# Another order and other PSUM banks in the attention loop of a hybrid decoder step (RetNet, RWKV-7, memory attention, MoE)

## The chip, the cores and the metric

One NeuronCore of one Trainium2 chip runs the whole program. The metric is the device time in microseconds of one execution; the kernel before is given by the median of three runs.

## What is computed

One decoder layer serves a prompt of 1024 tokens and 64 sample tokens (8 sequences of 8), model width 1024, all in float32. The change touches one of its stages, the attention over a memory of 256 tokens with 4 heads of 256, and what leads from there into the expert router:

```python
h = h + rmsnorm(h, g_mem_q) -> q @ w_mq, scores with mem_k * 256 ** -0.5, softmax, @ mem_v, @ w_mo
hn = rmsnorm(h, g_ffn)
gl = hn @ w_group_router + b_group_router        # 4 columns
el = hn @ w_expert_router + b_expert_router      # 32 columns
```

The prompt rows use keys and values projected from the prompt's memory; the sample rows use a cache of their own. Before this stage stand the combined projection and the two mixers, behind it the sorting of tokens by expert, the 32 experts and the sum of their outputs.

## The kernel before, in words

The program is a row of phases, each with engine programs written out by hand that are held together by semaphores: phase_project, phase_mixers, phase_attention, phase_route, phase_experts, phase_combine. A program for an engine runs in its written order; `wait_ge` holds the whole engine. PSUM is one tensor of eight banks; a 128 x 1024 float32 result takes two.

phase_attention (L1254 to L1983) first projects keys and values of the memory, multiplies the mixers' output by w_out, and then goes over the rows in tiles of 128: i = 0 to 7 are the prompt (NT = 8), i = 8 is the sample tile (TILES = 9). Large products with weights are made from float32 split into two halves that TensorE takes at a higher rate: ScalarE writes the high half (a_hi, o_hi), VectorE the rest (a_lo, o_lo), and TensorE adds three products (`terms`, L1759), 48 matmuls of 512 columns for each tile.

The steps of the loop over i, by the functions of the engines:
- scores(i) (L1835, TensorE): queries of tile i against kT, into banks 4 and 5.
- maxima(i) (L1500, VectorE), exps(i) (L1676, ScalarE), divide(i) (L1509, VectorE): the softmax into p.
- queries(i + 1) (L1815, TensorE): tile i + 1 times w_mq into banks 2 and 3. query_rows (L1659, ScalarE) scales them into the buffer rows; turn_q (L1827, TensorE) transposes them into banks 4 and 5; query_turned (L1668, ScalarE) copies them to qT.
- turn_p(i) (L1844, TensorE) transposes p into banks 0 and 1; p_turned(i) (L1685, ScalarE) copies it to bT.
- values(i) (L1852, TensorE): values by p, into banks 6 and 7. o_high (L1691, ScalarE) and o_low (L1514, VectorE) split the result.
- attend(i) (L1870, TensorE): times w_mo, into banks 2 and 3.
- back(i) (L1529, VectorE): adds it to h (L1532), takes the mean square (L1462, L1463), waits for POOL's reciprocal root (L1427) and writes the normed rows hn (L1539).
- turn_hn, hn_turned, router, logits (L1860, L1518, L1864, L1523) for tile i - 1, one iteration late: TensorE transposes hn into banks 0 and 1, VectorE copies it to bT (L1521), TensorE multiplies by the router's 36 columns (L1867) into bank 0, VectorE adds the bias (L1527).
- turn_h(i + 2) (L1804, TensorE), h_high (L1650, ScalarE), h_low (L1495, VectorE), front(i + 2) (L1486, VectorE): the next but one tile of h, turned into banks 4 and 5 and split, and its mean square.

All transposes are recorded at one line, L1756, in `turn`. bT serves both p and hn; qT holds the queries alone. SP's queue (L1393 to L1407) stores h (store_h2), stores hn (store_hn), loads the h of tile i + 3 (load_h1, L1329) and stores the logits of tile i - 1, in this order; behind queries(8) it asks for the cached sample keys (L1403).

TensorE's order in the loop is the one that the change rewrites:

```python
for i in range(NT):
    scores(i); queries(i + 1); turn_p(i); turn_q(i + 1); values(i)
    if i >= 1: turn_hn(i - 1)
    if i + 2 < TILES: turn_h(i + 2)
    if i >= 1: router(i - 1)
    attend(i)
```

VectorE's: maxima, divide, front(i + 2), o_low, hn_turned(i - 1), h_low(i + 2), logits(i - 1), back(i). ScalarE's: exps, query_rows(i + 1), p_turned, query_turned(i + 1), o_high, h_high(i + 2).

Behind the loop the sample tile is treated in another way (turn_cache, sample_scores, sample_values, L1880 to L1913); turn_hn(7) and router(7) stand within that part.

Of the kernel before, what the change touches and what calls it, by code (L numbers as in the profile page):

```python
# [1253 lines left out]
def phase_attention(core, PS):  # L1254
# [18 lines left out]
    with ExitStack() as ctx:  # L1273
# [27 lines left out]

        with nc.Block() as block:
# [142 lines left out]
            def _(v):  # L1445
# [49 lines left out]
                def h_low(i):  # L1495
                    par = (TILES + i) % 2
                    v.wait_ge(S_("h_high"), i + 1)
                    v.tensor_tensor(a_lo[:, par], two(4), as_f32(a_hi[:, par]), ALU.subtract).then_inc(S_("hT"), 1)
# [19 lines left out]
                def hn_turned(i):  # L1518
                    v.wait_ge(S_("hn_turned"), i + 1)
                    v.wait_ge(S_("valued"), min(i + 2, NT))  # L1520
                    v.tensor_copy(bT[:], two(0)).then_inc(S_("hnT"), 1)  # L1521

                def logits(i):  # L1523
# [3 lines left out]
                    v.tensor_tensor(lg[:], PS[:, 0, 0:NR], br[:], ALU.add).then_inc(S_("lg_ready"), 1)  # L1527

                def back(i):  # L1529
# [6 lines left out]
                    mean_square(h[:, n % HB], hn[:], st[:, 29:30], ms_c(1)).then_inc(S_("back_ms"), 1)  # L1536
                    v.wait_ge(S_("back_rstd"), i + 1)
# [44 lines left out]
                for i in range(NT):  # L1582
                    maxima(i, MH, 4)
                    divide(i, MH)
                    if i + 2 < TILES:
                        front(i + 2)
                    o_low(i)
                    if i >= 1:
                        hn_turned(i - 1)
                    if i + 2 < TILES:  # L1590
                        h_low(i + 2)
                    if i >= 1:
                        logits(i - 1)
                    back(i)
# [21 lines left out]
                back(NT)  # L1616
# [4 lines left out]
            def _(act):  # L1621
# [28 lines left out]
                def h_high(i):  # L1650
# [6 lines left out]
                    act.copy(a_hi[:, par], two(4)).then_inc(S_("h_high"), 1)  # L1657
# [10 lines left out]
                def query_turned(i):  # L1668
# [3 lines left out]
                    else:  # L1672
                        act.wait_ge(S_("split"), NPC * 5)
                    act.copy(qT[:], two(4)).then_inc(S_("qT"), 1)
# [10 lines left out]
                def p_turned(i):  # L1685
                    act.wait_ge(S_("p_turned"), i + 1)
                    if i >= 2:
                        act.wait_ge(S_("routed"), i - 1)
                    act.copy(bT[:], two(0)).then_inc(S_("pT"), 1)
# [37 lines left out]
                for i in range(NT):  # L1727
                    exps(i, MH, 4)
                    query_rows(i + 1)
                    p_turned(i)  # L1730
                    query_turned(i + 1)
                    o_high(i)
# [38 lines left out]
            def _(pe):  # L1771
# [32 lines left out]
                def turn_h(i):  # L1804
# [4 lines left out]
                    elif i == 1:  # L1809
                        pe.wait_ge(S_("hT"), 1)  # L1810
                    else:
                        pe.wait_ge(S_("qT"), i)
                    turn(pe, h[:, n % HB], 4).then_inc(S_("h_turned"), 1)
# [13 lines left out]
                def turn_q(i):  # L1827
# [3 lines left out]
                    else:  # L1831
                        pe.wait_ge(S_("hT"), 2)
# [822 lines left out]
```

## Time and profile before

| | |
|---|---|
| median of 3 runs | 2282.51 us (2279.8 to 2287.14) |
| profiled execution | 2281.6 us, span 2279.6 us |
| mean granted TensorE clock | 0.907 |
| TensorE matmuls busy | 1885.1 us, 83% of the span |
| VectorE / ScalarE / GpSimd busy | 53% / 37% / 14% |
| the loop over i = 1 to 7 | 1149.60 to 1423.25 us |

The span runs from the first to the last instruction of the profiled execution. Busy times of TensorE count matmuls, which are pipelined: they overlap a little, so that the next one starts before the one ahead is written as ended. Weight loads stand apart as PEld. The granted clock is 1.00 at 2.4 GHz and 0.50 at 1.2 GHz.

### The profile page before, as it was taken

What the parts mean: (1) busy time and instruction counts of PE and PEld (TensorE: products, weight loads), DVE (VectorE), ACT (ScalarE), POOL (GpSimd) and SP (SyncE); (2) the same over time, 40 slices, a digit from 0 to 9 for tenths busy, and PEclk for the clock granted to TensorE, in tenths of its full rate; (3) what the DMA queues carried; (4) which work ended last, traced back from release to release, by engine and by line L of the source; (5) the groups of instructions that cost most, each with busy time, mean ns of one, the idle gap of its engine ahead of it and who ended that gap; (6) DMA issues with size and microseconds to landing.
All of it is one profiled execution on the core that took longest, in us unless ns stands there. A gap on an engine that the chain in (4) does not pass through costs nothing. (4 is left out here: it accounts for less than half of the span.)

```text
span 2279.6 us, 36876 instructions
## 1 busy us (share of the span) xinstructions
PE 1885.1 (83%) x15456; PEld 1601.7 (70%) x15456; DVE 1219.1 (53%) x1285; ACT 843.9 (37%) x931; POOL 327.5 (14%) x283
## 2 busy tenths in 40 slices
PE   6999993677878877689999999860899999999950
PEld 5999993566667665578788887730688888888840
DVE  5201000668787873532433332213899999899935
ACT  4212110233333321420312121100677777777723
POOL 1000000323243332000000000003121111111004
PEclk9999997789998987799999999985899999999975
DMA  4322216721112201764111114403999999999928
GB/s 154 140 79 77 76 46 168 197 78 63 67 70 106 66 16 51 275 220 167 56 48 37 38 47 167 167 27 111 331 407 398 404 405 404 401 404 402 391 84 308
DMA packets 113144, 407.77 MB, mean 179 GB/s; under 512 B 27800, under 2 KB 50472, under 8 KB 84864
## 3 DMA queue, kind: packets, MB, share of 16 engines
q1 hardware_dynamic: 90256, 348.11, 41.6%
q10 hardware_dynamic: 14976, 32.12, 3.6%
q0 software_dynamic: 7792, 25.75, 3.0%
q8 instruction: 98, 1.61, 0.3%
q14 instruction: 22, 0.18, 0.0%
HBM read 345.84 MB, written 68.56 MB: 182 GB/s over the span
## 5 line engine op out<-in xcount | busy, mean ns | idle before, releaser
L2363 DVE TENSOR_TENSOR ex_w_lo<-moe_raw,ex_w_hi 128x2048 fp32r<-128x2048 f32 x192 | 431.1, 2284 | 97.9 <-ACT ex_w_hi L2428 97.7
L2428 ACT CAST ex_w_hi<-moe_raw 128x2048 fp32r<-128x2048 f32 x192 | 364.0, 1912 | 157.9 <-PE banks L2273 90.2
L2273 PE MATMUL banks<-ex_w_hi,ex_x_hi 128*128 128x512 f32 x512 | 208.1, 406 | 10.9 <-issue 5.4
L295 PE MATMUL banks<-pj_w_hi,pj_x_lo 128*128 128x416 f32 x576 | 204.3, 355 | 0.0
L295 PE MATMUL banks<-pj_w_hi,pj_x_hi 128*128 128x416 f32 x576 | 204.0, 354 | 0.0
L295 PE MATMUL banks<-pj_w_lo,pj_x_hi 128*128 128x416 f32 x576 | 202.3, 351 | 0.0
L2273 PE MATMUL banks<-ex_w_hi,ex_x_lo 128*128 128x512 f32 x512 | 202.1, 395 | 0.0
L2273 PE MATMUL banks<-ex_w_lo,ex_x_hi 128*128 128x512 f32 x512 | 201.5, 394 | 0.0
L199 DVE TENSOR_TENSOR pj_w_lo<-pj_w,pj_w_hi 128x3328 fp32r<-128x3328 f32 x8 | 29.0, 3623 | 221.4 <-ACT pj_w_hi L254 221.4
L247 ACT COPY pj_out<-banks 128x416 f32<-128x416 f32 x72 | 36.5, 507 | 255.3 <-PE banks L295 255.3
L2273 PEld LDWEIGHTS banks<-ex_w_hi,ex_x_hi 128*128 128x128 f32 x512 | 97.5, 190 | 42.8 <-issue 21.7
L2273 PEld LDWEIGHTS banks<-ex_w_hi,ex_x_lo 128*128 128x128 f32 x512 | 97.4, 190 | 21.3
L2273 PEld LDWEIGHTS banks<-ex_w_lo,ex_x_hi 128*128 128x128 f32 x512 | 97.7, 191 | 18.5
L295 PEld LDWEIGHTS banks<-pj_w_lo,pj_x_hi 128*128 128x128 f32 x576 | 109.3, 190 | 1.8
L295 PEld LDWEIGHTS banks<-pj_w_hi,pj_x_hi 128*128 128x128 f32 x576 | 109.1, 189 | 1.3 <-DVEq L217 0.6
L295 PEld LDWEIGHTS banks<-pj_w_hi,pj_x_lo 128*128 128x128 f32 x576 | 108.9, 189 | 0.7
L2273 PE MATMUL banks<-ex_w_hi,ex_h_hi 128*128 128x512 f32 x256 | 101.9, 398 | 6.0 <-DVE ex_h_lo L2375 6.0
L2273 PE MATMUL banks<-ex_w_hi,ex_h_lo 128*128 128x512 f32 x256 | 101.8, 398 | 0.0
L2273 PE MATMUL banks<-ex_w_lo,ex_h_hi 128*128 128x512 f32 x256 | 101.6, 397 | 0.0
L1427 POOL TENSOR_TENSOR at_st<-at_st,at_expo 128x1 f32<-128x1 f32 x18 | 9.8, 543 | 587.0 <-DVE at_st L1463 587.0
L951 PE MATMUL banks<-mx_TTT,mx_X 64*64 64x64 f32 x1344 | 80.7, 228 | 9.8 <-DVE mx_X L578 8.3
L2245 POOL COPY ex_idx<-moe_slot_tok 128x1 int32 (+1 forms) x32 | 25.2, 788 | 423.9 <-PE banks L2188 415.8
(370 smaller groups left out, 3937.7 us busy)
## 6 DMA issues: line engine op xcount, KB each, us to landing
moe_raw<-w_e_gate SPq DMA_DIRECT2D x64, 1024.0 KB, 7.9
moe_raw<-w_e_up SPq DMA_DIRECT2D x64, 1024.0 KB, 10.4
moe_raw<-w_e_down SPq DMA_DIRECT2D x64, 1024.0 KB, 14.1
blocks<-ex_y ACTq DMA_DIRECT2D x32, 512.0 KB, 7.6
proj<-pj_out ACTq DMA_DIRECT2D x72, 208.0 KB
pj_w<-w_in SPq DMA_DIRECT2D x8, 1664.0 KB, 7.9
mx_pin<-proj SPq DMA_DIRECT2D x8, 1664.0 KB, 7.0
h<-at_h SPq DMA_DIRECT2D x18, 512.0 KB, 2.6
```

The lines of the kernel that those rows point to most:

```text
L199: v.tensor_tensor(w_lo[:, par], w[:, par], as_f32(w_hi[:, par]), ALU.subtract).then_inc(S_("w_split"), 1)
L247: act.copy(out[:, b], PS[:, 4 + b, 0:W]).then_inc(S_("banked"), 1)
L295: ins = pe.matmul(PS[:, 4 + t % BUFS, 0:W], a[:, t, k, :], b[:, par, k, :], start=k == 0 and n == 0, stop=k == KC - 1 and n == len(pairs) - 1)
L951: return pe.matmul(out, a, b, start=start, stop=stop, skip_group_check=True)
L1427: po.tensor_tensor(rstd_c(par), ms_c(par), expo[:, 0:1], ALU.pow).then_inc(S_(kind + "_rstd"), 1)
L2245: po.tensor_copy(idx[:, bf:bf + 1], slot_tok[:, bass.ds(n, 1)]).then_inc(S_("idx"), 1)
L2273: ins = pe.matmul(out, a, b, start=first and i == 0, stop=final and i == 2)
L2363: v.tensor_tensor(w_lo[:, j], raw[:, j], as_f32(w_hi[:, j]), ALU.subtract).then_inc(S_("w_split"), 1)
L2428: act.copy(w_hi[:, j], raw[:, j]).then_inc(S_("w_high"), 1)
```

## The change

On TensorE, turn_hn(i - 1) moves from behind values(i) to ahead of turn_p(i), that is right behind queries(i + 1), and router(i - 1) from behind turn_h(i + 2) to right behind values(i). p is turned into banks 6 and 7 instead of 0 and 1; h of the tiles 0, 1 and from 2 on into banks 4, 6 and 0; the router writes bank 3 for the tiles up to 6, and attend(i) waits for the logits of tile i - 1. hn is copied to qT instead of bT for the tiles up to 6; that copy waits for scores(i + 1), and query_turned waits for the router. On VectorE, back is cut in two: back_sum (addition and mean square) stays at the end of iteration i, back_row (the normed rows) comes behind the maxima of iteration i + 1; the copy of hn moves ahead of front and o_low, and the logits ahead of h_low. On ScalarE, o_high moves ahead of query_turned. Some waits of turn_h, turn_q, scores and turn_p go.

```diff
@@ -1299,6 +1299,10 @@
         def own_head(hd, bank):
             return two(bank)[:, 2 * hd:2 * hd + 2, :].rearrange("p c (b x) -> p c b x", x=MH * DS)[:, :, :, hd * DS:(hd + 1) * DS]
 
+        h_bank = lambda i: (4, 6, 0)[min(i, 2)]
+        hnT = lambda i: qT if i < NT - 1 else bT
+        lg_bank = lambda i: 3 if i < NT - 1 else 0
+
         with nc.Block() as block:
             @block.sync
             def _(sp):
@@ -1495,7 +1499,7 @@
                 def h_low(i):
                     par = (TILES + i) % 2
                     v.wait_ge(S_("h_high"), i + 1)
-                    v.tensor_tensor(a_lo[:, par], two(4), as_f32(a_hi[:, par]), ALU.subtract).then_inc(S_("hT"), 1)
+                    v.tensor_tensor(a_lo[:, par], two(h_bank(i)), as_f32(a_hi[:, par]), ALU.subtract).then_inc(S_("hT"), 1)
 
                 def maxima(i, n, bank):
                     if i < NT:
@@ -1517,16 +1521,19 @@
 
                 def hn_turned(i):
                     v.wait_ge(S_("hn_turned"), i + 1)
-                    v.wait_ge(S_("valued"), min(i + 2, NT))
-                    v.tensor_copy(bT[:], two(0)).then_inc(S_("hnT"), 1)
+                    if i < NT - 1:
+                        v.wait_ge(S_("scores"), i + 2)
+                    else:
+                        v.wait_ge(S_("valued"), NT)
+                    v.tensor_copy(hnT(i)[:], two(0)).then_inc(S_("hnT"), 1)
 
                 def logits(i):
                     v.wait_ge(S_("routed"), i + 1)
                     if i:
                         v.wait_ge(S_("lg_stored"), 16 * i)
-                    v.tensor_tensor(lg[:], PS[:, 0, 0:NR], br[:], ALU.add).then_inc(S_("lg_ready"), 1)
-
-                def back(i):
+                    v.tensor_tensor(lg[:], PS[:, lg_bank(i), 0:NR], br[:], ALU.add).then_inc(S_("lg_ready"), 1)
+
+                def back_sum(i):
                     n = TILES + i
                     v.wait_ge(S_("attended"), i + 1)
                     lk(v.tensor_tensor(h[:, n % HB], h[:, n % HB], flat2(2), ALU.add))
@@ -1534,6 +1541,9 @@
                     if i:
                         v.wait_ge(S_("hn_stored"), 16 * i)
                     mean_square(h[:, n % HB], hn[:], st[:, 29:30], ms_c(1)).then_inc(S_("back_ms"), 1)
+
+                def back_row(i):
+                    n = TILES + i
                     v.wait_ge(S_("back_rstd"), i + 1)
                     by_row = lambda ap: ap.rearrange("p (q c) -> p q c", c=KC)
                     v.scalar_tensor_tensor(hn[:].rearrange("p (c q) -> p q c", c=KC), by_row(h[:, n % HB]), rstd_c(1), by_row(gf[:]),
@@ -1581,17 +1591,20 @@
                 front(1)
                 for i in range(NT):
                     maxima(i, MH, 4)
+                    if i >= 1:
+                        back_row(i - 1)
                     divide(i, MH)
+                    if i >= 1:
+                        hn_turned(i - 1)
                     if i + 2 < TILES:
                         front(i + 2)
                     o_low(i)
                     if i >= 1:
-                        hn_turned(i - 1)
+                        logits(i - 1)
                     if i + 2 < TILES:
                         h_low(i + 2)
-                    if i >= 1:
-                        logits(i - 1)
-                    back(i)
+                    back_sum(i)
+                back_row(NT - 1)
                 for b in range(DB):
                     v.wait_ge(S_("kc_turned"), MT * b + 1)
                     if b:
@@ -1613,7 +1626,8 @@
                         dst = slice(gq * NS // 2, (gq + 1) * NS // 2)
                         v.tensor_tensor(o_lo[:, 2 * hd:2 * hd + 2, dst].rearrange("p c (b t) -> p c b t", t=DS), own_head(hd, 6 * (1 - gq)),
                                         as_f32(o_hi[:, 2 * hd:2 * hd + 2, dst]).rearrange("p c (b t) -> p c b t", t=DS), ALU.subtract).then_inc(S_("os_low"), 1)
-                back(NT)
+                back_sum(NT)
+                back_row(NT)
                 hn_turned(NT)
                 logits(NT)
 
@@ -1654,7 +1668,7 @@
                         act.wait_ge(S_("mix_out"), NT + i)
                     else:
                         act.wait_ge(S_("queried"), i - 1)
-                    act.copy(a_hi[:, par], two(4)).then_inc(S_("h_high"), 1)
+                    act.copy(a_hi[:, par], two(h_bank(i))).then_inc(S_("h_high"), 1)
 
                 def query_rows(i):
                     act.wait_ge(S_("queried"), i + 1)
@@ -1671,6 +1685,8 @@
                         act.wait_ge(S_("scores"), i)
                     else:
                         act.wait_ge(S_("split"), NPC * 5)
+                    if i >= 2:
+                        act.wait_ge(S_("routed"), i - 1)
                     act.copy(qT[:], two(4)).then_inc(S_("qT"), 1)
 
                 def exps(i, n, bank):
@@ -1684,9 +1700,9 @@
 
                 def p_turned(i):
                     act.wait_ge(S_("p_turned"), i + 1)
-                    if i >= 2:
-                        act.wait_ge(S_("routed"), i - 1)
-                    act.copy(bT[:], two(0)).then_inc(S_("pT"), 1)
+                    if i:
+                        act.wait_ge(S_("valued"), i)
+                    act.copy(bT[:], two(6)).then_inc(S_("pT"), 1)
 
                 def o_high(i):
                     act.wait_ge(S_("valued"), i + 1)
@@ -1728,8 +1744,8 @@
                     exps(i, MH, 4)
                     query_rows(i + 1)
                     p_turned(i)
+                    o_high(i)
                     query_turned(i + 1)
-                    o_high(i)
                     if i + 2 < TILES:
                         h_high(i + 2)
                 for b in range(DB):
@@ -1806,11 +1822,9 @@
                     pe.wait_ge(S_(f"h_loaded{n % HB}"), 16 * (n // HB + 1))
                     if i == 0:
                         pe.wait_ge(S_("mixT"), TILES)
-                    elif i == 1:
-                        pe.wait_ge(S_("hT"), 1)
-                    else:
-                        pe.wait_ge(S_("qT"), i)
-                    turn(pe, h[:, n % HB], 4).then_inc(S_("h_turned"), 1)
+                    elif i == 2:
+                        pe.wait_ge(S_("h1_ready"), TILES)
+                    turn(pe, h[:, n % HB], h_bank(i)).then_inc(S_("h_turned"), 1)
 
                 def queries(i):
                     par = (TILES + i) % 2
@@ -1828,13 +1842,10 @@
                     pe.wait_ge(S_("q_ready"), i + 1)
                     if i:
                         pe.wait_ge(S_("exps"), i)
-                    else:
-                        pe.wait_ge(S_("hT"), 2)
                     turn(pe, rows, 4).then_inc(S_("q_turned"), 1)
 
                 def scores(i):
                     pe.wait_ge(S_("qT"), i + 1)
-                    pe.wait_ge(S_("hT"), min(i + 2, TILES))
                     for hd in range(MH):
                         for c in range(2):
                             ins = pe.matmul(PS[:, 4 + hd // 2, hd % 2 * NMEM:(hd % 2 + 1) * NMEM], qT[:, 2 * hd + c, :], kT[:, 2 * hd + c, :],
@@ -1843,11 +1854,7 @@
 
                 def turn_p(i):
                     pe.wait_ge(S_("p_ready"), i + 1)
-                    if i >= 2:
-                        pe.wait_ge(S_("lg_ready"), i - 1)
-                    elif i == 0:
-                        pe.wait_ge(S_("h1_ready"), TILES)
-                    turn(pe, p[:].rearrange("p h m -> p (h m)"), 0).then_inc(S_("p_turned"), 1)
+                    turn(pe, p[:].rearrange("p h m -> p (h m)"), 6).then_inc(S_("p_turned"), 1)
 
                 def values(i):
                     pe.wait_ge(S_("pT"), i + 1)
@@ -1864,7 +1871,7 @@
                 def router(i):
                     pe.wait_ge(S_("hnT"), i + 1)
                     for k in range(KC):
-                        ins = pe.matmul(PS[:, 0, 0:NR], bT[:, k, :], wr[:, k, :], start=k == 0, stop=k == KC - 1)
+                        ins = pe.matmul(PS[:, lg_bank(i), 0:NR], hnT(i)[:, k, :], wr[:, k, :], start=k == 0, stop=k == KC - 1)
                     ins.then_inc(S_("routed"), 1)
 
                 def attend(i):
@@ -1872,6 +1879,8 @@
                         pe.wait_ge(S_("split"), NPC * 5)
                     if i < NT:
                         pe.wait_ge(S_("oT"), i + 1)
+                        if i:
+                            pe.wait_ge(S_("lg_ready"), i)
                     else:
                         pe.wait_ge(S_("os_low"), 2 * MH)
                     for j in range(NPC):
@@ -1944,15 +1953,15 @@
                 for i in range(NT):
                     scores(i)
                     queries(i + 1)
+                    if i >= 1:
+                        turn_hn(i - 1)
                     turn_p(i)
                     turn_q(i + 1)
                     values(i)
                     if i >= 1:
-                        turn_hn(i - 1)
+                        router(i - 1)
                     if i + 2 < TILES:
                         turn_h(i + 2)
-                    if i >= 1:
-                        router(i - 1)
                     attend(i)
                 turn_cache(0)
                 for u in range(MT * DB):
```

## Rows read from the trace of the kernel before

**Rows 1.** The page: its head, and busy time, share of the span and instructions by engine.
```profile
span 2279.6 us, 36876 instructions
...
PE 1885.1 (83%) x15456; PEld 1601.7 (70%) x15456; DVE 1219.1 (53%) x1285; ACT 843.9 (37%) x931; POOL 327.5 (14%) x283
```

**Rows 2.** Windows: busy time by engine, granted clock, DMA share, GB/s; iterations of the loop.
```profile
1149.60:1423.25 273.65, 258.23 (x1337) 219.68 (x1335) 84.04 (x108) 47.93 (x90) 7.04 (x13) 0.94 0.19 70
1188.23:1225.29 37.06, 34.98 (x194) 29.90 (x192) 12.37 (x16) 6.99 (x13) 1.08 (x2) 1.00 0.12 44
1225.29:1265.48 40.19, 38.11 (x194) 32.48 (x193) 12.36 (x16) 6.99 (x13) 1.08 (x2) 0.92 0.12 40
```

**Rows 3.** Instructions by line, 1149.6 to 1423.3: busy, mean ns, idle ahead, releaser.
```profile
L1867 PE MATMUL banks<-at_wr,at_bT 128*128 128x36 f32 x112 | 17.2, 318 | 13.1 <-DVE at_bT L1521 13.1
```

**Rows 4.** Timeline, 1202 to 1214 (i = 2): start, duration, instruction, idle before it.
```profile
1202.60 1.03 PE L1756 MATMUL banks<-at_ident,at_p 128*128 128x128 f32 x8
1202.79 1.11 ACT L1666 ACTIVATE at_rows<-banks,at_st 128x1024 f32<-128x1024 f32 x1 [5.59 <-PE banks L1762]
1203.81 1.00 ACT L1689 COPY at_bT<-banks 128x1024 f32<-128x1024 f32 x1
...
1203.96 1.09 PE L1756 MATMUL banks<-at_ident,at_rows 128*128 128x128 f32 x8 [0.33 <-ACT at_rows L1666]
...
1204.89 3.81 PE L1856 MATMUL banks<-at_bT,at_v 128*128 128x128 f32 x32
...
1208.54 1.04 PE L1756 MATMUL banks<-at_ident,at_hn 128*128 128x128 f32 x8
1208.74 1.01 ACT L1695 CAST at_o_hi<-banks 128x1024 fp32r<-128x1024 f32 x1 [2.63 <-PE banks L1856]
...
1209.41 1.04 PE L1756 MATMUL banks<-at_ident,at_h 128*128 128x128 f32 x8
1209.79 1.23 DVE L1516 TENSOR_TENSOR at_o_lo<-banks,at_o_hi 128x1024 fp32r<-128x1024 f32 x1 [3.16 <-ACT at_o_hi L1695]
...
1210.93 1.21 DVE L1521 COPY at_bT<-banks 128x1024 f32<-128x1024 f32 x1
...
1212.19 1.98 PE L1867 MATMUL banks<-at_wr,at_bT 128*128 128x36 f32 x16 [1.75 <-DVE at_bT L1521]
...
1214.00 0.48 PE L1760 MATMUL banks<-at_x_hi,at_o_hi 128*128 128x512 f32 x1
...
1214.21 0.20 DVE L1527 TENSOR_TENSOR at_lg<-banks,at_br 128x36 f32<-128x36 f32 x1 [0.93 <-PE banks L1867]
```

**Rows 5.** Windows, columns as in rows 2: around routers and idle stretches.
```profile
1210.50:1214.00 3.50, 1.81 (x16) 1.81 (x17) 2.77 (x3) 1.00 (x1) 0.00 (x0) 1.00 0.00 0
1249.80:1256.60 6.80, 6.80 (x24) 5.83 (x24) 0.72 (x2) 0.00 (x0) 0.00 (x0) 0.52 0.00 0
...
1136.80:1138.30 1.50, 0.00 (x0) 0.00 (x1) 1.34 (x2) 1.04 (x2) 0.00 (x0) 1.00 0.00 0
1443.80:1445.60 1.80, 1.80 (x19) 1.76 (x18) 0.00 (x0) 1.01 (x1) 0.00 (x0) 1.00 0.00 0
```

**Rows 6.** Timeline, 1225 to 1236 (i = 3): scores and what VectorE does behind them.
```profile
1225.29 3.61 PE L1840 MATMUL banks<-at_kT,at_qT 128*128 128x256 f32 x16
...
1228.97 2.08 DVE L1539 SCALAR_TENSOR_TENSOR at_hn<-at_h,at_st,at_gf 128x1024 f32<-128x1024 f32 x1 [0.66 <-POOL at_st L1427]
1230.88 1.20 DVE L1506 TENSOR_REDUCE at_st<-banks 128x4 f32<-128x1024 f32 x1
...
1234.50 1.23 DVE L1512 TENSOR_TENSOR at_p<-at_p,at_st 128x1024 f32<-128x1024 f32 x1
```

**Rows 7.** Issues of DMAs, 1140 to 1380: count, KB, us to landing; then one line's, L1403.
```profile
at_h<-h SPq DMA_DIRECT2D x6, 512.0 KB, 4.4
...
L1403 SPq DMA_DIRECT2D at_slots<-cache_mem_k x8: 333/449/787, 1399.0 to 1402.7; - x8
...
DMA to landing us min/median/max: 4.9/13.2/20.0
```

## What the change will do to the time

> **What bounds the kernel now.** I read the page first: a span of 2279.6 us in which TensorE's matmuls are busy for 83% and no other engine for more than 53% [rows 1]. The share says little about one stage, so I went to the stage that the diff touches, the attention loop over the eight prompt tiles, and cut it where attend(i - 1) ends and scores(i) begins. The view of windows gives the seven iterations with i = 1 to 7 together 273.65 us, at a mean granted clock of 0.94; the one with i = 2 takes 37.06 us at 1.00, the one with i = 3 takes 40.19 us at 0.92 [rows 2]. VectorE and ScalarE work for 12.37 and 6.99 us of the 37.06, TensorE for 34.98: the loop is bound by TensorE's own order of work, its few idle stretches, and its clock.
>
> The grouped instructions of the loop say where it idles: 13.1 us in front of the router's matmuls (L1867), released by VectorE's copy L1521 [rows 3], some 1.75 us in each iteration. The timeline shows why. TensorE turns the last tile's normed rows (at_hn) at 1208.54, then turns h, and stands from 1210.45 to 1212.19. VectorE can't copy the turned rows before o_low (1209.79 to 1211.02), which is ahead of the copy in its own order; the copy runs 1210.93 to 1212.14 and the router starts behind it [rows 4]. A smaller stretch of 0.33 us lies in front of the turned queries, which wait for ScalarE's rows (1202.79 to 1203.90).
>
> The windows also show the clock. In the iteration with i = 3 it is at half rate, 1.2 GHz, over most of 1249.80 to 1256.60 (0.52), from just behind the idle stretch, through the router, into attend; between 1210.50 and 1214.00, behind an idle stretch of the same length, it stays at 2.4 GHz (1.00); it also does at 1136.80 to 1138.30 (i = 0: idle, with no router behind it) and at 1443.80 to 1445.60 (the last prompt tile's router between transposes, with no idle stretch ahead) [rows 5]. So half rate comes where an idle stretch and the router's 36-column matmuls stand together, and not each time. Its price is a difference of rows: 273.65 - 7 x 37.06 = 14.2 us over the seven iterations.
>
> **The change part by part.** I count from t = 0, where the first transpose behind the queries starts (1202.60 in rows 4). Matmuls overlap a little, so I use start to start.
>
> 1. TensorE's new order: at_hn turned, p turned, queries turned, values, router, h turned, attend. A transpose group takes 0.87 us start to start (1208.54 to 1209.41). So p is turned from 0.87 to 1.90. ScalarE's rows are ready at 1.30 as before (1203.90), ahead of TensorE, which turns them from 1.74: the 0.33 us of idling goes. ScalarE copies p from 1.94 to 2.94; values starts 0.08 us later as now (1204.81 to 1204.89), at 3.02. TensorE would be free at 1.74 + 0.93 = 2.67, so 0.35 us of idling comes back in front of values, on the path.
>
> 2. VectorE's copy of the turned at_hn now goes to the buffer qT and stands ahead of front and o_low: 1.0 to 2.2, long before the router asks. Values takes 3.65 us start to start, so the router starts at 6.67 with no wait and ends at 8.65 (1.98 us), h is turned from 8.48, and TensorE is ready for attend at 8.48 + 0.88 = 9.36.
>
> 3. Attend has two conditions. Its old one, o_low: values ends at 6.83, ScalarE's cast takes 1.01 from 6.87, VectorE's subtraction 1.22 from 7.92 [rows 4], end 9.15. Its new one, the logits, because the router now writes bank 3, which attend overwrites. The logits stand behind o_low on VectorE, take 0.20 us, and are done between 9.1 and 9.35. Both land within 0.05 us of 9.36. Attend starts at 9.4 at the latest, against 1214.00 - 1202.60 = 11.40 now: 2.0 us less. What would be late next is these two together. For i = 7 there is no h to turn, and the same two conditions set 9.4. Seven iterations: 7 x 2.04 = **14.3 us**. Iteration 0 turns no at_hn and has no router, so it gains nothing.
>
> 4. Maxima ahead of the norm's last step. Scores end at 1228.90, but the maxima start at 1230.88, behind L1539 (2.08 us) [rows 6]. Now they start 0.1 us behind the scores and the exponents some 1.9 us earlier; the row step runs while ScalarE takes exponents, 5.2 to 7.3 us behind the start of scores. Division then ends near 8.6 instead of 10.4 (1235.73). TensorE asks for p 14 to 15 us behind the start of scores (1202.60 - 1188.23 = 14.4): worth nothing, since the queries cover it. The normed rows are ready at 7.3 and are now asked for at 14.4; if that cover went, p would be late first.
>
> 5. SP's queue. The store of at_hn waits for the row step, and the load of h for tile i + 2 stands behind it: the rows are ready 7.3 us behind the start of scores, now 5.8 (1231.05), so the load is issued 1.5 us later, near 8. It lands some 4.4 us behind its issue [rows 7], by 12.5; VectorE's front asks at about 17.2, the turn of h at 22.8. Nothing on the path. POOL's two powers keep their order.
>
> 6. ScalarE's queue. o_high goes ahead of the queries' copy, which now waits for the router (qT holds at_hn until then): done at about 9.7, asked for by the next scores at 9.4 + 11.3 = 20.7. Behind it stands h_high, 10.7 at the end, and h_low behind that; queries asks for them three to four us later still than the scores. Hidden, with some 11 us in hand. The other banks and the waits dropped in turn_h, turn_q and scores save only waits that had long been met: nothing in the rows of the loop waits there.
>
> 7. Behind the loop the order is the old one. The sample keys are asked for when the last queries are done, at 1399.0, and land 4.9 to 20.0 us later [rows 7]; attend(7) ends 24.3 us behind that request (1423.25) and would end 9.4 + 11.3 = 20.7 us behind it. Eight keys are used one after the other, the first of them at once, the last tens of us later, so none is late. The rest shifts as a whole.
>
> 8. **The clock.** The trace does not show this router with 36 columns directly behind values and ahead of a turn, at the end of an unbroken stretch. Bounds: nothing regained (0), or all of it (14.2 us). The nearest row is the router at 1443.80 to 1445.60, between transposes with no idle ahead of it, at 1.00 [rows 5]. Idling ahead of it falls from 1.75 us to 0, and the 0.35 us left lies in front of values. I take the upper bound, **14.2 us**.
>
> The Trainium skill (TensorE: Matmul & The Clock Gate, "HAM oscillation") speaks against term 8: it ties the return to half rate to long idle waits, such as for a DMA between bursts of matmuls, and an idle stretch as short as the one here would not cause it. By that rule the sum would hold term 3 alone. The half rate directly behind a stretch of 1.75 us disagrees with it. The page's next section knows a second way, short idling between groups of matmuls, and these rows fit that one better.
>
> Sum: 14.3 + 14.2 = 28.5 us. The profiled execution took 2281.6 us (2279.6 us of span and 2.0 around it), 0.9 below the median shown; 2281.6 - 28.5 = 2253.1, and from the median **2254.0 us**.
>
> **The rivals.** (a) The idle goes, the clock does not come back. For: the same turns and router, at few columns, still stand in one stretch. Against: rows 5, where this router without an idle stretch kept 1.00. Time: 2282.5 - 14.3 = 2268.2 if none comes back, 2261 if half. Chance 0.20. This is where the first rule of the Trainium skill's page above would leave the time.
>
> (b) A new wait keeps part of the gap: attend behind the logits, which stand behind o_low on VectorE. In the sum they arrive level; a delay of 1 us in each iteration costs 7, giving 2261 with the clock back and up to 2275 without. Chance 0.06.
>
> (c) The change does not do what it says: the copy is early but the stretch only moves, say to values, whose p now comes one turn later. The sum has 0.35 us there; only 2 us would take back the gain. Time 2279 to 2286. Chance 0.03.
>
> (d) Slower. The stretch from the first turn to attend becomes 9.4 us of work with few columns, and if the half rate takes it whole and runs on into attend as it now does, it costs more than it saves. An iteration with the longest half rate lost 40.19 - 37.06 = 3.1 us. It must lose over 28.5 / 7 = 4.1 us in each to end slower; twice the present worst, 6.2, gives 2254 + 43 = 2297. Against: no idle is added, and half rate was never longer than 6.8 us. Chance 0.04.
>
> **How the numbers follow.** The forecast has a chance of 0.67 with a range of its own of 2249 to 2259: seven iterations within 0.3 us each, and one period of half rate more or less in the tail. The range reaches to rival (a) in full and takes in the clock's lower bound: 2249 to 2269. A measurement of this kernel tells about 0.3%, 6.8 us, from no change. Forecast, (a) and (b) lie beyond it: faster 0.93; (c) 0.03; slower 0.04.
>
> **What would show it.** In the changed profile: each iteration with i = 1 to 7 takes 35.0 us at a granted clock of 1.00; idle in front of L1867 is near 0 instead of 13.1 us, and some 2.5 us in all stands in front of values (7 x 0.35); the maxima start 0.1 us behind the scores; attend starts 9.4 us behind the first turn, released by o_low or the logits. Wrong would be: half rate at the router or in attend with no idle ahead of it (rival a), TensorE waiting for L1527 by more than 0.3 us (b), or iterations above 37 us.

## The result, and the profile after

The changed kernel takes 2250.24 us (median of 4 runs, 2246.71 to 2252.59), the kernel before beside it 2281.16 us (median of 4): a ratio of 0.9865 with a 95% interval of 0.9841 to 0.9888, 30.9 us less. The forecast was 2254.0 us, 28.5 less than the median of before that it started from (2282.51 us).

The two profiled executions, 2281.6 and 2248.6 us, are 33.0 us apart. Of that, 28.2 us lie in the seven iterations of the loop: 273.65 us before [rows 2], 245.45 now. Another 4.8 us lie ahead of the attention phase, in code that is the same: its first load is issued at 914.40 us in the one trace and at 909.62 in the other. The seven iterations start at 1149.60 us in the first profile of before, at 1144.55 in this one, and between 1140.05 and 1146.59 in the eleven profiles below, behind code that does almost the same work; between 300 and 900 us the mean granted clock is 0.87 in the one trace and 0.88 in the other. This difference is not the change's.

Windows of the changed kernel (busy time of TensorE's matmuls, its weight loads, VectorE, ScalarE and GpSimd, then granted clock, DMA share and GB/s): the seven iterations, then those with i = 2 and 7.

```profile
1144.55:1390.00 245.45, 243.00 (x1337) 208.14 (x1335) 85.28 (x108) 48.08 (x90) 7.02 (x13) 1.00 0.21 77
...
1179.60:1214.64 35.04, 34.81 (x194) 29.88 (x192) 12.55 (x16) 7.00 (x13) 1.08 (x2) 1.00 0.13 47
1354.78:1390.00 35.22, 34.14 (x185) 28.91 (x183) 9.95 (x12) 6.08 (x12) 0.54 (x1) 1.00 0.63 259
```

Against [rows 2]: the iteration takes 35.0 us and not 37.06 to 40.2, and the clock is 1.00 over the whole stretch. Of 245.45 us, TensorE is busy for 243.00.

Timeline of the changed kernel in the iteration with i = 2, from the first transpose behind the queries to the start of attend, the stretch that answers to [rows 4]:

```profile
1193.96 1.03 PE L1772 MATMUL banks<-at_ident,at_hn 128*128 128x128 f32 x8
1194.16 1.12 ACT L1680 ACTIVATE at_rows<-banks,at_st 128x1024 f32<-128x1024 f32 x1 [7.52 <-PE banks L1778]
1194.84 1.04 PE L1772 MATMUL banks<-at_ident,at_p 128*128 128x128 f32 x8
1195.04 1.22 DVE L1528 COPY at_qT<-banks 128x1024 f32<-128x1024 f32 x1 [6.92 <-PE banks L1772]
1195.71 1.04 PE L1772 MATMUL banks<-at_ident,at_rows 128*128 128x128 f32 x8
1195.91 1.01 ACT L1705 COPY at_bT<-banks 128x1024 f32<-128x1024 f32 x1 [0.63 <-PE banks L1772]
...
1196.97 3.84 PE L1863 MATMUL banks<-at_bT,at_v 128*128 128x128 f32 x32 [0.23 <-ACT at_bT L1705]
...
1200.65 1.87 PE L1874 MATMUL banks<-at_wr,at_qT 128*128 128x36 f32 x16
1200.85 1.01 ACT L1711 CAST at_o_hi<-banks 128x1024 fp32r<-128x1024 f32 x1 [3.93 <-PE banks L1863]
1201.89 1.22 DVE L1520 TENSOR_TENSOR at_o_lo<-banks,at_o_hi 128x1024 fp32r<-128x1024 f32 x1 [3.58 <-ACT at_o_hi L1711]
1202.36 1.07 PE L1772 MATMUL banks<-at_ident,at_h 128*128 128x128 f32 x8
...
1203.04 0.18 DVE L1534 TENSOR_TENSOR at_lg<-banks,at_br 128x36 f32<-128x36 f32 x1
1203.37 0.47 PE L1776 MATMUL banks<-at_x_hi,at_o_hi 128*128 128x512 f32 x1
```

Counted from 1193.96, attend starts at 9.41 us; it was 11.40. The copy of hn (L1528) is done 1.08 to 2.30 us behind the first turn and the router asks for it at 6.69. The router itself follows the values with nothing between.

What TensorE waits for in the loop, from the grouped instructions of the changed kernel (busy, mean ns, idle ahead, releaser):

```profile
L1776 PE MATMUL banks<-at_x_hi,at_o_hi 128*128 128x512 f32 x112 | 45.0, 402 | 0.8 <-DVE at_lg L1534 0.8
...
L1863 PE MATMUL banks<-at_bT,at_v 128*128 128x128 f32 x224 | 26.9, 278 | 1.6 <-ACT at_bT L1705 1.6
L1874 PE MATMUL banks<-at_wr,at_qT 128*128 128x36 f32 x112 | 13.1, 274 | 0.0
```

The 13.1 us in front of the router [rows 3] are gone; 1.6 us now stand in front of values (seven times 0.23), and 0.8 us once in front of attend, behind the logits, in the last iteration, which has no h to turn.

### The profile page after: what moved, and what is told of

Read it like the earlier page. It is cut to its first block and busy times, and to the rows that moved or that the text cites. A ratio compares the mean times of both kernels' runs of the same rounds, so it can differ in the third digit from the quotient of the medians.

```text
span 2246.6 us, 36862 instructions
## 1 busy us (share of the span) xinstructions
PE 1863.1 (83%) x15456; PEld 1584.5 (71%) x15456; DVE 1220.4 (54%) x1285; ACT 843.6 (38%) x931; POOL 327.6 (15%) x283
```

## The experiments

Eleven kernels ran, four or more times each, all beside runs of the kernel before. Two questions were open. Is the half of the gain that came with the clock really caused by the idle stretch that went, and what in it counts? And do the parts that were costed at nothing cost nothing? Since the stages ahead of the loop move by some microseconds between executions, the sharper reading is the length of the seven iterations, from the start of scores(1) to the end of attend(7), beside the length of one iteration at full clock. The last iteration, which turns no h, is 0.2 us longer than the others where no half rate falls (35.22 against 35.04 us above), so each excess over seven such lengths holds about 0.2 us that is not half rate.

**The changed kernel again.**

> The changed kernel once more, as the mark for the other three runs of this chip. Both theories: 2250 us, some 31 us under the kernel before; the seven iterations 245.5 us at a granted clock of 1.00.

Measured: 2251.53 us (median of 5) beside 2281.95, ratio 0.987 (0.9845 to 0.9895). The window of the seven iterations:

```profile
1146.01:1391.48 245.47, 243.03 (x1337) 208.15 (x1335) 85.29 (x108) 48.11 (x90) 7.04 (x13) 1.00 0.21 77
```

245.47 us here, 245.45 in the first profile: the loop came out alike in both profiles of this kernel.

**One step of the order alone.** In the kernel before:

```diff
-                    o_low(i)
                     if i >= 1:
                         hn_turned(i - 1)
+                    o_low(i)
```

> The kernel before with one step of VectorE's order moved: the copy of the turned hn stands ahead of o_low. TensorE's order is the old one. By the sum, the copy runs 7.0 to 8.2 us behind the first turn, the router starts at 8.3 (now 9.59) and attend at 10.1 (now 11.40): 1.3 us less in each of seven iterations, 9.1 us. Theory (half rate comes from the idle stretch next to the router, which shrinks from 1.75 to about 0.45 us): another 14 us, in all 2258 us, iterations of 35.8 us at 1.00. Rival (the clock came back by TensorE's new order or the banks): 2272 us, clock near 0.94 in the iterations.

Measured: 2256.43 us, ratio 0.9894 (0.987 to 0.9917). Windows, the seven iterations and the one with i = 2:

```profile
1143.03:1395.07 252.04, 245.75 (x1337) 209.46 (x1335) 83.41 (x108) 47.91 (x90) 7.02 (x13) 0.99 0.20 76
1178.78:1214.54 35.76, 34.99 (x193) 29.91 (x192) 12.26 (x16) 6.99 (x13) 1.08 (x2) 1.00 0.13 46
```

The router's row in the grouped instructions of the loop:

```profile
L1867 PE MATMUL banks<-at_wr,at_bT 128*128 128x36 f32 x112 | 13.8, 281 | 4.0 <-DVE at_bT L1521 4.0
```

The iteration came out at 35.76 us where 35.8 was expected, and half rate costs 252.04 - 7 x 35.76 = 1.7 us over the seven. The idling is 0.44 us in each of the first six iterations, 1.31 in the last, and the half rate lies in the last alone (37.47 us). One step moved in VectorE's order, with TensorE's order and all banks as before, brings 25.5 us of the 30.4 on that chip (21.6 of 28.2 in the loop). The rival falls: the clock needs neither the new order of TensorE nor the banks.

**The clock alone.** In the kernel before, useless work in the idle stretch; banks 2 and 3 are free there:

```diff
                     if i >= 1:
+                        turn(pe, hn, 2)
+                        turn(pe, hn, 2)
                         router(i - 1)
```

> The kernel before, with two useless transposes of hn (2 x 0.87 us) into banks 2 and 3 in the idle stretch ahead of the router: nothing starts earlier. Theory: the granted clock of the iterations goes from 0.94 to 1.00 and that alone brings 14 us: 2267 us, iterations of 37.1 us. Rival (the clock depends on something else than this idle stretch, or falls as it likes): 2281 us, iterations of 37 to 40 us.

Measured: 2264.48 us, ratio 0.9927 (0.9906 to 0.9949): 17.5 us less, by doing more. Windows as above:

```profile
1144.99:1404.61 259.62, 256.41 (x1449) 220.53 (x1447) 84.08 (x108) 47.97 (x90) 7.03 (x13) 1.00 0.20 74
1182.05:1219.12 37.07, 36.74 (x210) 31.66 (x209) 12.38 (x16) 7.00 (x13) 1.08 (x2) 1.00 0.12 44
```

Six iterations take 37.06 or 37.07 us, the length of the one undisturbed iteration of [rows 2], and the last 37.23; the seven are 273.65 - 259.62 = 14.0 us shorter than before. The router starts where it did, so this is the price of the half rate, and it goes when TensorE no longer stands there. Whether standing is the whole of the cause, the runs on the router's columns ask below. The 17.5 us between the medians (interval 11.6 to 21.5) agree with 14.0; the rest is not accounted for.

**The same, half filled.** One `turn(pe, hn, 2)` instead of two. The theories A and B named in the expectation belong to the router's columns, further below: A asks for an idle stretch and work with few columns near it, B for the idle stretch alone.

> The kernel before with one useless transpose group of 0.87 us in the idle stretch ahead of the router, which leaves 0.88 us of it. Nothing starts earlier. Theory A and B alike: less idle, so fewer iterations with half rate than before; between 2267 us (none) and 2281 us (as before). If an idle stretch of half the length is enough for half rate, it is nearer to the latter.

Measured: 2269.61 us, ratio 0.9964 (0.9952 to 0.9976). The window of the loop and the router's row:

```profile
1141.12:1406.98 265.86, 256.53 (x1393) 219.26 (x1391) 84.07 (x108) 47.90 (x90) 7.02 (x13) 0.97 0.19 72
```
```profile
L1867 PE MATMUL banks<-at_wr,at_bT 128*128 128x36 f32 x112 | 14.5, 288 | 7.0 <-DVE at_bT L1521 7.0
```

With 7.0 us of idling instead of 13.1, half rate costs 265.86 - 7 x 37.07 = 6.4 us instead of 14.2. With the exchanged lines it was 4.0 us of idling and 1.7 us of half rate. The lengths of the single iterations in these traces say where it fell. Among i = 1 to 6, half rate touched five of six with 1.75 us of idling ahead of the router (the kernel before), two of six with 0.87 us (this run), none of six with 0.44 us (the exchanged lines). The last iteration turns no h and stands 0.87 us longer: it was touched with 2.62, 1.75 and 1.31 us, and not with 0.87 (two groups of filler). Less idling makes half rate rarer, then; this is one profile of each kernel.

**One part undone: the early maxima.** In the changed kernel:

```diff
                     maxima(i, MH, 4)
-                    if i >= 1:
-                        back_row(i - 1)
                     divide(i, MH)
...
                     back_sum(i)
-                back_row(NT - 1)
+                    back_row(i)
```

> The changed kernel without one part: the norm's last step stands at the end of its iteration again, ahead of the next maxima. Theory (p and hn are ready 5 us before TensorE asks, either way): no difference from the changed kernel, 2250 to 2252 us, iterations of 35.0 us. Rival (the early maxima carry part of the gain): 2 us in each iteration, 2265 us.

Measured: 2249.79 us, ratio 0.9864 (0.9847 to 0.9882), and the same loop:

```profile
1143.56:1389.05 245.49, 243.05 (x1337) 208.18 (x1335) 84.59 (x108) 48.11 (x90) 7.05 (x13) 1.00 0.21 77
```

In the loop this part of the change is worth 0.0 us.

**The idle stretch put back ahead of the router.** In the changed kernel, with front also ahead of hn_turned again:

```diff
                 def hn_turned(i):
                     v.wait_ge(S_("hn_turned"), i + 1)
+                    v.wait_ge(S_("valued"), min(i + 2, NT))
                     if i < NT - 1:
-                        v.wait_ge(S_("scores"), i + 2)
-                    else:
-                        v.wait_ge(S_("valued"), NT)
+                        lk(v.tensor_copy(hnT(i)[:, 0:4], two(0)[:, 0:4]))
                     v.tensor_copy(hnT(i)[:], two(0)).then_inc(S_("hnT"), 1)
...
+                    if i + 2 < TILES:
+                        front(i + 2)
                     if i >= 1:
                         hn_turned(i - 1)
-                    if i + 2 < TILES:
-                        front(i + 2)
```

> The changed kernel with an idle stretch put back ahead of the router: VectorE's copy of hn waits for the values again and half of it is done twice. The router starts at about 8.9 instead of 6.67 us, 2.0 us of them idle. Both theories: 2.2 us more in each of seven iterations, 15.6 us. Theory (idle next to the router brings half rate): up to 14 us on top, 2275 to 2280 us, clock of the iterations 0.92 to 0.96. Rival (new order or banks keep the clock up): 2266 us at 1.00.

Measured: 2282.21 us beside 2279.98, ratio 1.0007 (0.9997 to 1.0017). The loop and the router's row:

```profile
1142.13:1421.68 279.55, 262.80 (x1337) 225.63 (x1335) 90.14 (x115) 48.68 (x90) 7.05 (x13) 0.93 0.18 69
```
```profile
L1873 PE MATMUL banks<-at_wr,at_qT 128*128 128x36 f32 x112 | 20.3, 352 | 14.8 <-DVE at_qT L1527 14.8
```

The loop is 34.1 us longer than in the changed kernel. The router starts 2.27 us later behind the start of scores (23.32 against 21.05), 2.11 of them idle: 15.9 us of delay over seven iterations, where 15.6 were expected. That leaves 18.2 us for the half rate, above the 14 expected; all seven iterations are touched (38.85 to 40.47 us). The new order with the old fault has lost all its gain; the router's matmuls themselves are slower (352 against 274 ns).

**The idle stretch ahead of attend.** In the changed kernel:

```diff
                 def o_low(i):
                     v.wait_ge(S_("o_high"), i + 1)
+                    if i:
+                        lk(v.tensor_tensor(o_lo[:], two(6), as_f32(o_hi[:]), ALU.subtract))
+                        lk(v.tensor_tensor(o_lo[:, 0:4], two(6)[:, 0:4], as_f32(o_hi[:, 0:4]), ALU.subtract))
```

> The changed kernel with VectorE's subtraction for attend done one and a half times more: TensorE idles about 1.9 us ahead of attend, behind the turn of h, which stands between it and the router. 2.0 us more in each of seven iterations, 14 us, so 2264 us. Theory (the router must be next to the idle stretch): clock 1.00, 2264 to 2268 us. Rival (an idle stretch of this length suffices wherever it lies): clock 0.92 to 0.96, 2275 to 2279 us.

Measured: 2275.89 us beside 2279.98, ratio 0.9977 (0.9965 to 0.9989). Windows: the loop, the iterations with i = 2 and i = 3; then TensorE's timeline at the start of attend in each of these two.

```profile
1146.59:1415.55 268.96, 253.00 (x1337) 215.42 (x1335) 98.12 (x122) 48.07 (x90) 7.03 (x13) 0.96 0.19 71
1184.95:1221.98 37.03, 34.88 (x194) 29.88 (x192) 14.38 (x18) 7.00 (x13) 1.08 (x2) 1.00 0.13 44
1221.98:1261.75 39.77, 37.62 (x193) 31.93 (x192) 14.38 (x18) 7.00 (x13) 1.08 (x2) 0.91 0.12 41
```
```profile
1210.69 0.47 PE L1779 MATMUL banks<-at_x_hi,at_o_hi 128*128 128x512 f32 x1 [1.92 <-DVE at_lg L1537]
1211.01 0.39 PE L1780 MATMUL banks<-at_x_lo,at_o_hi 128*128 128x512 f32 x1
...
1247.72 0.77 PE L1779 MATMUL banks<-at_x_hi,at_o_hi 128*128 128x512 f32 x1 [1.93 <-DVE at_lg L1537]
1248.29 0.63 PE L1780 MATMUL banks<-at_x_lo,at_o_hi 128*128 128x512 f32 x1
```

The delay is as expected (37.03 - 35.04 = 2.0 us in each), but half rate came too, in five of the seven iterations: 268.96 - 7 x 37.03 = 9.8 us. The stated theory falls: the router need not touch the idle stretch. The two starts of attend show how alike the cases are: the same 1.92 and 1.93 us of idling, then matmuls of 0.39 us in one and 0.63 us in the other.

**The idle stretch behind the router.** As above, with the orders of TensorE's last turns exchanged:

```diff
-                    if i >= 1:
-                        router(i - 1)
                     if i + 2 < TILES:
+                        if i >= 1:
+                            pe.wait_ge(S_("hnT"), i)
                         turn_h(i + 2)
+                    if i >= 1:
+                        router(i - 1)
                     attend(i)
```

> As the run before it, but h is turned ahead of the router: attend starts at the same time, and the idle stretch of about 1.9 us lies directly behind the router. Theory (idle and router together): half rate in most iterations, clock 0.92 to 0.96, 2272 to 2279 us. Rival (the idle stretch must lie ahead of the router): as the run before, 2264 us at 1.00.

Measured: 2277.52 us, ratio 0.9986 (0.9976 to 0.9995), and the loop:

```profile
1145.44:1418.74 273.30, 257.15 (x1337) 219.17 (x1335) 98.69 (x122) 48.08 (x90) 7.03 (x13) 0.94 0.19 70
```

273.30 - 7 x 37.03 = 14.1 us of half rate, in all seven iterations. So the idle stretch need not lie ahead of the router. Directly beside it, half rate was more frequent than with a turn between (14.1 against 9.8 us in one profile each), but the medians are only 1.6 us apart with intervals that overlap, so this difference is not shown.

**The router's columns.** In the kernel before, each of the router's matmuls takes 128 columns; the buffer of its weights is 92 columns longer, with zeros, and the logits stay in the first 36:

```diff
-                        ins = pe.matmul(PS[:, 0, 0:NR], bT[:, k, :], wr[:, k, :], start=k == 0, stop=k == KC - 1)
+                        ins = pe.matmul(PS[:, 0, 0:P], bT[:, k, :], wrp[:, k * NR:k * NR + P], start=k == 0, stop=k == KC - 1)
...
```

> The kernel before with a wider router: each of its matmuls takes 128 columns instead of 36 (the next columns of the same weights and zeros behind them; the 36 logits are the same). Its sixteen passes start as often as those of the values, which have 128 columns too, so they should take 1.9 to 2.0 us as now; the idle stretch ahead of it stays at 1.75 us. Theory A (half rate needs the idle stretch and work with few columns near it): 1.00 in most iterations, 37.1 us each, 2267 to 2270 us. Theory B (what counts is the time that TensorE stands, whatever the router is): 2280 us, clock 0.94 as before.

Measured: 2266.41 us beside 2277.85, ratio 0.9945 (0.9927 to 0.9963). The windows of the loop and of i = 2, and the router's row:

```profile
1142.82:1404.06 261.24, 245.82 (x1337) 209.79 (x1335) 84.20 (x108) 47.91 (x90) 7.04 (x13) 0.99 0.19 73
1179.89:1216.96 37.07, 34.99 (x194) 29.91 (x193) 12.39 (x16) 6.99 (x13) 1.08 (x2) 1.00 0.13 44
```
```profile
L1869 PE MATMUL banks<-at_wr,at_bT 128*128 128x128 f32 x112 | 15.4, 295 | 13.1 <-DVE at_bT L1523 13.1
```

TensorE still stands for 13.1 us ahead of the router, and an iteration still takes 37.07 us, but half rate costs 261.24 - 7 x 37.07 = 1.7 us instead of 14.2. All of it lies in the last iteration (38.84 us), where TensorE stands for 2.62 us; with 1.75 us none of the other six is touched, where five were before. So standing alone is not it: that the router's matmuls are narrow is the other part of the cause here. More arithmetic in the same number of matmuls made the kernel 11 us faster.

**The same in the kernel with the idle stretch ahead of attend.**

> The run with the idle stretch ahead of attend, with the same wider router. There the half rate came although the turn of h stood between router and idle stretch. Theory A: the granted clock of the iterations is 1.00, and the time goes from 2276 to 2264 us. Theory B: it stays at 2276 us.

Measured: 2267.52 us, ratio 0.9959 (0.9943 to 0.9976), and the loop:

```profile
1140.05:1402.47 262.42, 246.79 (x1337) 210.76 (x1335) 98.23 (x122) 48.10 (x90) 7.05 (x13) 0.99 0.20 73
```

262.42 - 7 x 37.03 = 3.2 us of half rate instead of 9.8, in two iterations (i = 4 and 7) instead of five. This second run is the weaker one: the executions lie between 2260.51 and 2271.70 us, the profile is of the fastest of them, and the ratio (0.9943 to 0.9976) overlaps the one with the narrow router (0.9965 to 0.9989). B is out by the run before, where it stated 2280 us and 2266.41 were measured; that A needs no contact between router and idle stretch rests on this run's one profile beside the narrow router's.

The traces hold two more cases that nobody set up. In iteration 0, which has no router, TensorE stands for 1.58 us ahead of attend in each of the thirteen profiles, and half rate follows in none of them. But the start of iteration 0 has no router near it either, and there half rate came in six of the thirteen (35.8 to 36.0 us instead of 34.3). In the kernel before, the timeline of TensorE, then a window:

```profile
1111.54 1.06 PE L1756 MATMUL banks<-at_ident,at_rows 128*128 128x128 f32 x8 [1.25 <-issue]
1113.70 5.29 PE L1840 MATMUL banks<-at_kT,at_qT 128*128 128x256 f32 x16 [1.10 <-ACT at_qT L1674]
```
```profile
1114.00:1116.50 2.50, 2.50 (x7) 1.94 (x7) 0.15 (x1) 0.00 (x0) 0.56 (x1) 0.50 0.00 0
```

Two idle stretches with eight transposes between them are enough there. The router is therefore one kind of work that brings half rate beside idling, not the only one. Which other work does the same was not tried.

**A faster version.** In the changed kernel:

```diff
                     queries(i + 1)
+                    turn_p(i)
                     if i >= 1:
                         turn_hn(i - 1)
-                    turn_p(i)
                     turn_q(i + 1)
...
                     back_sum(i)
-                back_row(NT - 1)
...
                     v.tensor_copy(kcT[:, 0], two(2)).then_inc(S_("kcT0"), 1)
+                    if b == 0:
+                        back_row(NT - 1)
...
-                    rstd_of("back", 1, i + 1)
+                    if i < NT - 1:
+                        rstd_of("back", 1, i + 1)
...
+                rstd_of("back", 1, NT)
                 rstd_of("back", 1, TILES)
```

> The changed kernel with p turned ahead of hn, so that ScalarE's copy of p is done before TensorE asks for it, and behind the loop VectorE's first copy of the sample keys and POOL's clearing of the values' buffer ahead of the last norm. Theory: 0.35 us less in each of seven iterations (34.7 instead of 35.05) and 2.4 us less ahead of the first sample scores, 4.8 us in all: 2245 us. Rival (the two conditions of attend, o_low and logits, now hold it back; the tail waits for something else): 2249 to 2250 us.

Measured: 2242.67 us, ratio 0.9829 (0.9807 to 0.9852), 8.9 us under the changed kernel on the same chip. The loop:

```profile
1145.82:1387.84 242.02, 241.18 (x1337) 207.99 (x1335) 84.72 (x108) 47.30 (x90) 9.81 (x18) 1.00 0.21 77
```

And GpSimd's last reciprocal root of the phase, in this kernel and then in the changed one, as a mark near the end of the tail:

```profile
1483.25 0.54 POOL L1431 TENSOR_TENSOR at_st<-at_st,at_expo 128x1 f32<-128x1 f32 x1 [91.92 <-DVE at_st L1469]
```
```profile
1488.58 0.54 POOL L1431 TENSOR_TENSOR at_st<-at_st,at_expo 128x1 f32<-128x1 f32 x1 [92.30 <-DVE at_st L1467]
```

The loop is 3.4 us shorter (0.5 in each iteration, where 0.35 was expected: values start 0.39 us earlier behind the first turn, and the router 0.11 more), and from the end of attend(7) to the mark it is 95.4 us instead of 98.6, 3.2 us less where 2.4 was expected. That is 6.6 of the 8.9 us; the rest is not accounted for. In the loop TensorE is now busy for 241.18 of 242.02 us: little is left there but its own work.

## Why the prediction was right, point by point

1. TensorE's new order. Stated: values at 3.02 us behind the first turn, router at 6.67, attend at 9.36 to 9.4. Measured: 3.01, 6.69 and 9.41. The idling put in front of values came out at 0.23 us and not 0.35: the queries' turn, now behind another transpose group, ends 0.12 us later than the start-to-start count made it. It changes nothing, since values starts when ScalarE's copy is done. The start of attend is right in part by luck: the router took 1.71 us start to start (1.81 stated, between 6.67 and 8.48), and attend came 1.01 us behind the first transpose of h instead of 0.88.

2. and 3. The copy of hn is early, and o_low and the logits arrive level with TensorE. The logits end at 1203.22 and attend starts at 1203.37, so the new wait is the tightest point, as stated. Rival (b) had its place right and a small price: by the 0.87 us of a transpose group TensorE would have been free 9.27 us behind the first turn, so the logits held it for some 0.14 us, an estimate, 1 us over seven iterations. The term: 7 x 2.04 = 14.3 us stated; 7 x (37.06 - 35.04) = 14.1 measured.

4. Maxima. In the changed kernel VectorE does this behind the scores, which end at 1183.22 there:

```profile
1183.25 1.23 DVE L1510 TENSOR_REDUCE at_st<-banks 128x4 f32<-128x1024 f32 x1 [0.62 <-PE banks L1851]
...
1184.59 2.08 DVE L1549 SCALAR_TENSOR_TENSOR at_hn<-at_h,at_st,at_gf 128x1024 f32<-128x1024 f32 x1
...
1186.89 1.22 DVE L1516 TENSOR_TENSOR at_p<-at_p,at_st 128x1024 f32<-128x1024 f32 x1
```

The division ends 8.5 us behind the start of scores (8.6 stated) and is asked for at 14.4 or later: no effect, and undoing this part showed none.

5. to 7. SP's queue, ScalarE's queue and the tail: no wait of TensorE in the loop but the two of the rows above. From the end of attend(7) to the end of the span it is 2279.6 - 1423.25 = 856.4 us before and 2246.6 - 1390.00 = 856.6 after.

8. The clock. All 14.2 us were taken, and all came: the loop's excess over seven undisturbed iterations is 14.2 us before and 0.2 after, which is the longer last iteration. The filler run, which starts the router no earlier, puts the price at 14.0 us. The reason given was right in its two parts, an idle stretch (the filler) and few columns (the wider router), but narrower than what the runs show: the prediction tied half rate to the idle stretch and the router standing together, and it also came with a turn between them, and at the start of iteration 0 with no router at all. The prediction had the row of that iteration's later idle stretch [rows 5] and not this one. Taking the whole 14.2 us was a choice between two bounds that rested on one row, of this router without idling; it held. The first rule weighed there, of the Trainium skill (TensorE: Matmul & The Clock Gate, "HAM oscillation"), which ties half rate to long idle waits, would have left term 3 alone; the filler run disagrees with it by 14 us. The next section of that page of the Trainium skill, on short idling between groups of matmuls, agrees with the half rate that ran here beside idle stretches of 1.75 us.

The sum against the result: 28.5 us stated, 28.2 in the profiled loop, 30.9 between the medians, whose interval (0.9841 to 0.9888) reaches from 25.5 to 36.3 us. The 2.7 us between the last two are not accounted for and lie within it. Rival (d), slower, needed over 4.1 us of half rate in each iteration; there was none.

## What to carry to other kernels

Before costing an idle stretch of TensorE at its length, look at the granted clock behind it: here 13.1 us of idling cost another 14.2 us in slow matmuls, and the place to look is where idling falls among work with few columns. Count a reordering from the first instruction that moves, with each engine's own queue beside it, and look for the smallest step that removes the wait: moving one step of VectorE's order brought 25.5 of 30.4 us. Where the wait can't be removed, filling it with useless transposes gave back all that the clock had taken in the loop (14.0 us), and widening the narrow matmul most of it (12.4 us).

## What the runs showed of the hardware

- Useless work can shorten a kernel: 112 added transposes, 14.0 us off the loop at 37.07 us an iteration.
- A router of 128 columns costs per matmul nearly what one of 36 costs (295 ns mean against 318 before, part of those at half rate; 275 against 274 ns in the two kernels with the idle stretch ahead of attend), and with it the clock of the loop was 0.99, with the same idle stretch that stands beside 0.94 in the kernel before.
- The same idle stretch in the same kernel brings no half rate in one iteration and brings it in the next (1.92 and 1.93 us of idling, 37.03 and 39.77 us an iteration). What decides between them was not tried; the loop that has no such stretch also came out within 0.02 us in its two profiles (245.45 and 245.47 us).
- The share of iterations with half rate falls with the idling ahead of the router: five of six with 1.75 us, two of six with 0.87, none of six with 0.44, in one profile of each kernel.
- Half rate needs no 36-column matmul: it came behind 1.25 and 1.10 us of idling around eight transposes, in six of thirteen profiles.
